# Moving the recurrent mixer of a two-block transformer kernel into the third attention

## Chip, cores and metric

One NeuronCore of one Trainium2 chip. The metric is the device time of one execution in microseconds. The engines are TensorE (PE: matmuls and transposes), VectorE (DVE), ScalarE (ACT), GpSimd (POOL) and the DMA queues, here fed by SyncE (SP). Each runs its own list of instructions in order and waits on semaphores for the others.

## What is computed

One sequence of 512 tokens of width 1024, all in float32, goes through three layers. Layers 0 and 1 add a gated residual; layer 2 is a mixer of three kinds, cut here to what the change touches.

```python
# layer 0 (even): latent attention (8 heads) and windowed attention with sinks (8 heads)
# layer 1 (odd):  differential attention (4 pairs) and forgetting attention (8 heads)
o = concat(o_a, o_b) * silu(z_gate);  x = x + gate * rmsnorm(o @ w_out, g_post)

# layer 2: sparse attention (6 heads: compressed, selected, window), stick-breaking (4 heads), recurrent (6 heads)
def hgrn2_mixer(q, f_logit, i_val, lb):            # chunks of 64 tokens
    def step(state, inp):
        b = cumsum(lf); decay = where(causal, exp(b_t - b_s), 0)
        att = einsum('bhtd,bhsd,bhtsd->bhts', qx, kx, decay)
        o = att @ vx + (qx * exp(b)) @ state
        state = exp(b_last) * state + (kx * exp(b_last - b)).T @ vx
o_hg = o_hg * rsqrt(mean(o_hg**2) + 1e-6) * hg_norm_w
mixed = concat(o_nsa * silu(nsa_z), o_sb * silu(sb_z), o_hg * silu(hg_z))
x = layer_norm(ALPHA * x + mixed @ w_out, ln_g, ln_b)
```

## The kernel before

The tokens are four tiles of 128 rows (`T = 4`). Weights come in chunks of 512 columns (2 MB) through a ring of three slots (`ring`, `ring_slots`); SyncE issues each chunk's load when the chunk that held its slot before has been used. `pr_plan` writes out the list of jobs (projections, transposes, output products) that TensorE runs in this order.

An attention (`attention(L)` on each engine) is a list of steps, one for each head and token tile: 64 steps in layer 0, 48 in layer 1, 88 in layer 2. In step v TensorE makes the scores of two steps ahead (`LOOK = 2`, two banks `SC`), transposes the weights of step v (`PT`) and multiplies those of step v - 1 with the values (`OB`). VectorE adds the mask and takes the maximum, ScalarE takes the exponential and copies the transposed weights. For differential and compressed attention VectorE also combines the weights before the transposes (semaphore `post`).

Between these, TensorE runs *fill*: projections that later stages need, cut into single products. `FILLERS[L]` lists the jobs, `SPREAD[L]` says over how many steps each few of them are dealt, and `UNITS` how many products a job counts. Half of a step's fill stands before its transposes and half behind. All fill jobs take two PSUM banks in turn (`PR`; `few` in `two_block_kernel`), so a job waits until the job two places before it has been copied out, which VectorE or ScalarE does in `tile_done`, at the end of the step in which the job ended. A gate job (`silu`) takes a clamp on VectorE, three exponentials on ScalarE (`exp_neg`) and a product on VectorE (`finish_gates`, in the next step).

In attention 1 (layer 0) the fill is a cycle of four steps: a gate tile of eight products (`gate0`), a strip of the modulation product (`adas`, its weights loaded into one slot) and the column sum of the strip before it (`adac` or `adag`). Then come the output products of the finished token tiles (`finish_tile`: two transposes `mT`, two results `y` of eight products each) and the transposed input of the next layer (`hT`). The last token tile of each layer is finished behind the attention (`last_tile`).

In layer 2 the steps are compressed, selected and window attention for token tiles 0 to 3, then the 16 stick-breaking steps. The recurrent mixer stands behind them, tile by tile: GpSimd takes the differences of the running sums for six levels of block sizes and multiplies the exponentials with keys and queries (`differences`, `operands`, 15 and 16 instructions), ScalarE takes the exponentials (`exponentials`), TensorE makes the gram products of a pair of heads (`level_products`), VectorE multiplies them with the level masks and adds the levels (seven instructions for a pair), TensorE multiplies with the values and the state (`outputs`), VectorE norms (one chain of ten instructions), and the output products of the tile before run beside it (`output_tile`). The final layer norm takes two passes on ScalarE, small steps on VectorE, and its last multiply and add on GpSimd. Below, "attention 1, 2, 3" are `attention(0)`, `attention(1)`, `attention(2)`.

## Time and profile before

| what | us |
|---|---|
| median of 3 runs | 1437.36 |
| the 3 runs | 1437.36, 1437.13, 1442.88 |
| the profiled execution, its own time | 1442.61 |
| its span (first to last instruction on the core) | 1441.1 |
| TensorE busy | 1264.0 (88%) |
| VectorE busy | 554.3 (38%) |
| ScalarE busy | 427.3 (30%) |
| GpSimd busy | 113.7 (8%) |
| stages by start: attention 1, 2, 3, stick steps, recurrent part | 194.3, 588.5, 966, 1230, 1299.8 |

Busy times overlap, so they don't add up to the span. The span says what one profiled execution took on the core; the runs' times are taken without the profiler.

### The profile page before, as it was taken

To read this page: it belongs to the slowest core of one execution; us is meant where nothing else is said; L and a number is where in the kernel's file an instruction comes from. 1 tells how busy PE (TensorE), PEld (TensorE's weight loads), DVE (VectorE), ACT (ScalarE), POOL (GpSimd) and SP (SyncE) were. 2 spreads that over 40 slices of the span, in tenths; PEclk is the share of its full clock that TensorE was granted. 3 is DMA by queue.
4 is the path that set the end of the run, shared out by engine and by line. 5 is a ranking of instruction groups with operands and counts; after the bars stand their busy time and mean duration, and the time that the engine had idled before them with its cause. 6 is when DMAs were issued, how large, how long until landed. Compare 5 with 4: busy or idle time off the path is not lost.

```text
span 1441.1 us, 15111 instructions
## 1 busy us (share of the span) xinstructions
PE 1264.0 (88%) x5264; PEld 699.6 (49%) x5264; DVE 554.3 (38%) x1422; ACT 427.3 (30%) x1086; POOL 113.7 (8%) x140
## 2 busy tenths in 40 slices
PE   4889986899998999889999989989998999856974
PEld 1555543445564444334455555555454545545541
DVE  3233322333544520334442432112125731667871
ACT  0133022334432201322234332114233533651211
POOL 0000000000001000000000000000000000484722
PEclk9989997999998999999999999989999999966986
DMA  9222334444000432322111004241101111000000
GB/s 349 92 81 64 112 117 172 146 175 118 1 1 1 117 59 59 52 67 58 59 59 59 1 11 131 59 161 44 45 0 45 44 59 59 1 0 31 1 30 29
DMA packets 60258, 99.71 MB, mean 69 GB/s; under 512 B 12068, under 2 KB 22129, under 8 KB 60184
## 3 DMA queue, kind: packets, MB, share of 16 engines
q1 hardware_dynamic: 54370, 93.58, 20.8%
q10 hardware_dynamic: 5814, 5.18, 1.1%
q8 instruction: 43, 0.70, 0.2%
q14 instruction: 31, 0.25, 0.1%
HBM read 96.60 MB, written 4.08 MB: 70 GB/s over the span
## 4 chain that ended last, share of the span: by engine, by line
PE 72%; DVE 14%; ACT 5%; issue 3%; DMA 3%; POOL 2%; ACTq 1%; DVEq 0%; SPq 0%; POOLq 0%
PE PR L856 29%; PE SC L908 6%; PE OB L886 6%; PE PT L768 6%; PE PR L768 4%; PE OB L768 4%; PE SC L768 4%; PE PT L923 3%; PE PR L949 3%; DMA ring<-in_w_ada 3%; DVE d L1661 2%; DVE stage L1661 2%; POOL arena L1569 2%; DVE tok L1661 1%; DVE arena L1877 1%
## 5 line engine op out<-in xcount | busy, mean ns | idle before, releaser
L856 PE MATMUL PR<-ring,hT 128*128 128x512 f32 (+1 forms) x784 | 381.2, 599 | 9.3 <-DVE arena L1817 6.3
L1349 ACT ACTIVATE stage<-stage,nmax 128x256 f32<-128x256 f32 (+7 forms) x200 | 103.7, 519 | 335.3 <-DVE nmax L1981 311.2
L856 PEld LDWEIGHTS PR<-ring,hT 128*128 128x128 f32 x784 | 136.3, 198 | 114.4 <-issue 98.4
L886 PEld LDWEIGHTS OB<-arena,pts 128*128 128x128 f32 (+3 forms) x880 | 132.2, 202 | 97.4 <-issue 75.9
L908 PE MATMUL SC<-arena 64*128 64x256 f32 (+15 forms) x432 | 147.5, 452 | 10.0 <-DVE nmax L1981 10.0
L856 PE MATMUL PR<-hT,ring 128*128 128x512 f32 (+1 forms) x304 | 152.8, 626 | 0.0
L1569 POOL TENSOR_TENSOR arena<-arena 128x192 f32<-128x192 f32 (+1 forms) x118 | 80.5, 683 | 826.1 <-PE OB L886 778.2
L886 PE MATMUL OB<-arena,pts 128*128 128x64 f32 (+4 forms) x880 | 131.0, 278 | 9.2 <-ACT pts L1197 9.2
L923 PEld LDWEIGHTS PT<-ident,stage 128*128 128x128 f32 (+3 forms) x440 | 58.2, 145 | 131.0 <-issue 65.1
L923 PE MATMUL PT<-ident,stage 128*128 128x128 f32 (+3 forms) x440 | 87.5, 290 | 34.7 <-ACT stage L1328 15.9
L1197 ACT ACTIVATE pts<-PT 128x256 f32<-128x256 f32 (+7 forms) x200 | 80.7, 404 | 58.4 <-issue 22.2
L1981 DVE CUSTOM_DVE_ANT_0 stage<-SC,causal 128x128 f32<-128x128 f32 (+3 forms) x96 | 47.2, 491 | 113.4 <-issue 61.4
L856 PEld LDWEIGHTS PR<-hT,ring 128*128 128x128 f32 (+1 forms) x304 | 51.6, 191 | 56.1 <-issue 54.8
L908 PEld LDWEIGHTS SC<-arena 64*128 64x128 f32 (+2 forms) x432 | 61.4, 191 | 25.4 <-DVE nmax L1981 10.4
L1981 DVE CUSTOM_DVE_ANT_0 stage<-SC,arena 128x128 f32<-128x128 f32 (+7 forms) x72 | 28.0, 388 | 116.8 <-issue 59.5
L949 PE MATMUL PR<-ring,hT 128*128 128x512 f32 x128 | 64.0, 655 | 5.9 <-DVE hT L2205 5.9
L768 PE MATMUL PR<-ring,hT 128*128 128x512 f32 (+5 forms) x160 | 48.9, 460 | 3.9 <-ACT hT L1240 2.0
L768 PE MATMUL PT<-ring,hT 128*128 128x512 f32 (+4 forms) x144 | 50.0, 502 | 0.0
L768 PE MATMUL SC<-ring,hT 128*128 128x512 f32 (+3 forms) x144 | 47.9, 490 | 0.0
L1665 DVE TENSOR_SCALAR t<-PR 128x512 f32<-128x512 f32 (+3 forms) x29 | 17.4, 600 | 73.2 <-PE PR L856 62.0
L949 PEld LDWEIGHTS PR<-ring,hT 128*128 128x128 f32 x128 | 26.1, 211 | 36.4 <-issue 30.0
L1217 ACT ACTIVATE t<-t 128x512 f32<-128x512 f32 (+3 forms) x32 | 16.8, 525 | 79.2 <-DVE t L1665 79.2
(337 smaller groups left out, 1306.6 us busy)
## 6 DMA issues: line engine op xcount, KB each, us to landing
ring<-in_w_ada SPq DMA_DIRECT2D x12, 2048.0 KB, 8.8
ring<-in_od_w_in SPq DMA_DIRECT2D x8, 2048.0 KB, 14.6
ring<-in_w_in SPq DMA_DIRECT2D x5, 1536.0 KB, 6.8
ring<-in_ev_w_in SPq DMA_DIRECT2D x3, 2048.0 KB, 7.7
ring<-in_w_in SPq DMA_DIRECT2D x3, 2048.0 KB, 9.8
ring<-in_ev_w_out SPq DMA_DIRECT2D x2, 2048.0 KB, 10.1
ring<-in_od_w_out SPq DMA_DIRECT2D x2, 2048.0 KB, 8.7
ring<-in_w_out SPq DMA_DIRECT2D x2, 2048.0 KB, 7.8
```

The costliest lines, as they stand in the source:

```text
L768: mm = pe.matmul(dst, lhs(k), rhs(k), start=(k == 0), stop=(k == K - 1))
L856: mm = pe.matmul(dst, l, r, start=(k == 0), stop=(k == KT - 1))
L886: mm = pe.matmul(ob[:, h * w:h * w + w], pts[0:rows_, v % 2, n * P:n * P + P], vb, start=(n == 0), stop=(n == len(blocks) - 1))
L908: pe.matmul(SC[s % 2][:, 0:n], q, k, start=True, stop=True).then_inc(s_done, 1)
L923: tr = pe.transpose(PT[v % 2][0:w, b * P:b * P + P], pb[:, s % NP, b * P:b * P + w], ident[:, :])
L949: mm = pe.matmul(b[:, :], hT[:, k, i * P:i * P + P], W[:, k, :], start=(k == 0), stop=(k == KT - 1))
L1197: return act.activation(dst, src, ACT.Copy, scale=scale)
L1349: give(act.activation(pb[:, s % NP, 0:n], zm[:, s % 2, 0:n], ACT.Exp, bias=nmax[:, row, c:c + 1], scale=-1.0, accum_out=rsum[:, row, c:c + ...
L1569: return pool.tensor_tensor(dst, a, b, op)
L1661: return dve.tensor_tensor(dst, a, b, op)
L1665: return dve.tensor_scalar(dst, a, s1, None, op0)
L1981: give(dve.tensor_tensor_reduce(out=z, in0=SC[s % 2][:, 0:n], in1=mask, scale=-scale, scalar=start, op0=ALU.add, op1=ALU.min, accum_out=nm ...
```

## The change

1. The recurrent mixer becomes fill of attention 3. Its jobs (`kbT`, `gram`, `ho`, `st`) and the output products of token tiles 0 to 2 go into `FILLERS[2]`; the stick steps come behind the first token tile. Gram products and level sums go head by head, the levels are added by one `tensor_reduce` over a transposed view, and the head norm, the layer norm and the exponentials become chains that advance once a step. The slot of the chunk `nz` is kept out of the ring and holds the first set of GpSimd's operands; the second set overlays the stick arrays.
2. In all three attentions VectorE's order within a step becomes: finish the gates, combine the weights, mask, and then what is left of the step before (group norms, chains, `tile_done`). Only `mT` and `hT` jobs are still handled in their own step (`URGENT`). ScalarE likewise handles the step before between its exponentials and its copy.
3. Half of each last token tile (four of eight transposes and of each result's eight products) becomes fill (`last_ahead`, `output_half`). `SPREAD` deals the fill anew.
4. The layer norm's last multiply and add of the last tile move from GpSimd to VectorE, in halves that are written out one by one.

```diff
+AHEAD = {0: 0, 1: 0, 2: 1}
+def last_ahead(L):
+    return [("mT", L, T - 1, AHEAD[L])], [("ahead", L, 0), ("ahead", L, 1)]
...
-     (("w", "hz"), [("hz", i) for i in range(T)]),
      (("w", "hq"), [("hq", m) for m in range(3)]),
-     (("w", "hi"), [("hi", i) for i in range(T)])],
+     (("w", "hi"), [("hi", i) for i in range(T)]),
+     (("w", "hz"), [("hz", 0), ("hz", 1)]),
+     (("wo", 2, 0), []),
+     (("wo", 2, 1), []),
+     (("w", "hz"), [("kbT", 0)] + grams(0, 0, 2) + [("hz", 2)] + grams(0, 2, 5) + [("hz", 3)]),
+     (("wo", 2, 1), grams(0, 5, 6) + [("ho", 0), ("st", 0), ("kbT", 1)] + grams(1, 0, 6) + finish_tile(2, 0)[:2]
+      + [("ho", 1), ("st", 1)] + finish_tile(2, 0)[2:3] + grams(2, 0, 1) + finish_tile(2, 0)[3:] + [("kbT", 2)]
+      + grams(2, 1, 2) + finish_tile(2, 1)[:3] + grams(2, 2, 3) + finish_tile(2, 1)[3:] + grams(2, 3, 6)
+      + [("ho", 2), ("st", 2), ("kbT", 3)] + grams(3, 0, 6) + [("ho", 3)] + finish_tile(2, 2)
+      + last_ahead(2)[0] + last_ahead(2)[1])],
...
-SPREAD = [[(4, 5)] + [(3, 4)] * 6 + [(5, 9), (2, 1), (4, 10), (2, 1), (2, 9), (2, 5)], [(15, 15), (4, 12), (4, 8), (2, 1), (2, 5), (2, 1), (2, 1), (2, 5)], [(21, 68), (4, 14)]]
+SPREAD = [[(4, 5)] + [(3, 4)] * 6 + [(5, 9), (2, 1), (4, 10), (2, 1), (2, 7), (2, 1), (1, 1), (2, 5)], [(15, 14), (4, 11), (1, 1), (2, 1), (2, 7), (2, 1), (2, 6), (2, 1), (2, 1), (4, 5)], [(11, 15), (12, 18), (2, 1), (2, 2), (1, 1), (1, 1), (2, 2), (1, 1), (1, 2),
+           (2, 1), (2, 1), (1, 1), (2, 1), (1, 1), (2, 1), (1, 1), (2, 3), (2, 3), (2, 1), (2, 1), (2, 3), (2, 3), (2, 1),
+           (1, 2), (2, 1), (1, 1), (1, 1), (1, 1), (2, 1), (1, 1), (1, 2), (2, 1), (1, 3), (1, 3), (1, 1), (2, 5)]]
...
+EXP_STEPS = (26, 38, 46, 56)
...
+            def level_sums(c, h):
+                b, w = take(dve, ("gram", c, h)), att[h]
+                link(tt(gm, b[:, 0:GW], levels, ALU.mult))
+                release(dve.tensor_copy(w[0:HB, HB:P], b[0:HB, GW:GW + HB]), ("gram", c, h))
+                link(dve.tensor_reduce(w[:, 0:HB], gm.rearrange("p (l t) -> p t l", l=NLEV), AX.X, ALU.add))
+                give(dve.tensor_copy(w[HB:P, HB:P], w[HB:P, 0:HB]), gs_s, HGH * c + h + 1)
...
+                def finish_behind(v, done):
+                    if late_group:
+                        finish_group(*late_group.pop(), part=1)
+                    if v >= 1 and v_units[v - 1][0] == L and last_v[L, v_units[v - 1][1]] == v - 1:
+                        finish_group(L, v_units[v - 1][1])
+                    for chain in chains:
+                        next(chain, None)
+                    for name in done:
+                        if name[0] not in URGENT:
+                            tile_done(name)
+                behind = None
                 for r_, (v, (_, g, j, sus), new) in enumerate(steps(L)):
+                    done = schedule[L][1][r_] if r_ < len(schedule[L][1]) else []
+                    finish_gates()
+                    if r_:
+                        finish_weights(v, g, sus)
                     for s in new:
...
+                    if behind:
+                        finish_behind(*behind)
+                    if urgent(done):
+                        finish_gates()
+                    for name in urgent(done):
+                        tile_done(name)
+                    behind = (v, done)
```

## Rows read from the trace of the kernel before

**Rows 1.** stages: each engine's busy us (instructions), granted clock (PEclk), DMA share.

```profile
194.30:449.60 255.30, 222.79 (x954) 124.32 (x952) 95.90 (x262) 98.51 (x272) 2.92 (x1) 0.91 0.29 96
...
588.50:859.80 271.30, 251.25 (x905) 131.12 (x903) 106.78 (x285) 84.82 (x215) 0.00 (x0) 0.98 0.17 47
...
966.00:1230.00 264.00, 252.70 (x927) 136.50 (x928) 91.98 (x282) 103.47 (x285) 0.00 (x0) 0.97 0.12 40
...
1230.00:1299.80 69.80, 50.83 (x199) 32.78 (x197) 45.64 (x68) 42.02 (x81) 46.79 (x62) 0.78 0.00 1
...
1299.80:1441.10 141.30, 100.36 (x973) 60.71 (x973) 90.98 (x189) 24.10 (x47) 59.55 (x71) 0.79 0.06 23
```

**Rows 2.** timeline, stick steps: start, us, engine, line, operation [idle before <-releaser].

```profile
1289.50 1.11 PE L923 MATMUL PT<-ident,stage 128*128 128x128 f32 x4 [7.43 <-ACT stage L1328]
```

**Rows 3.** timeline, TensorE, gram products of one pair of heads.

```profile
1316.47 1.21 PE L1116 MATMUL PT<-arena 64*64 64x64 f32 x56
```

**Rows 4.** timeline, TensorE, the last tile of attention 1.

```profile
449.65 1.08 PE L783 MATMUL SC<-ident,tok 128*128 128x128 f32 x4 [3.03 <-DVE tok L1661]
...
461.54 7.03 PE L856 MATMUL OB<-ring,hT 128*128 128x512 f32 x16
```

**Rows 5.** timeline, the end of the kernel.

```profile
1426.90 0.69 DVE L1669 SCALAR_TENSOR_TENSOR ring<-x,PR 128x512 f32<-128x512 f32 x1 [6.15 <-PE PR L949]
...
1435.45 2.34 POOL L1569 TENSOR_TENSOR x<-ring,arena 128x1024 f32<-128x1024 f32 x1
```

**Rows 6.** timeline, GpSimd, differences and products of a tile's decays.

```profile
1231.85 10.42 POOL L1569 TENSOR_TENSOR arena<-arena 128x192 f32<-128x192 f32 x15 [778.22 <-PE OB L886]
...
1286.94 11.07 POOL L1569 TENSOR_TENSOR arena<-arena 128x192 f32<-128x192 f32 x14 [4.02 <-ACT arena L1385]
...
1298.09 2.07 POOL L1569 TENSOR_TENSOR ring<-ring,arena 128x384 f32<-128x384 f32 x2
```

**Rows 7.** timeline, VectorE, level sums, head norm, and the sums again beside GpSimd.

```profile
1303.38 1.09 DVE L1661 TENSOR_TENSOR stage<-SC,grow 128x896 f32<-128x896 f32 x1 [2.19 <-PE SC L1119]
...
1304.83 1.21 DVE L1661 TENSOR_TENSOR stage<-stage 128x384 f32<-128x384 f32 x3
...
1306.08 0.61 DVE L1661 TENSOR_TENSOR ring<-stage 64x128 f32<-64x128 f32 x2
...
1314.62 0.56 DVE L2239 COPY d<-OB 128x384 f32<-128x384 f32 x1 [1.27 <-PE OB L1137]
...
1315.81 0.55 DVE L2241 TENSOR_REDUCE fr<-d 128x6 f32<-128x384 f32 x1
...
1320.44 0.75 DVE L1661 TENSOR_TENSOR tok<-tok,d 128x384 f32<-128x384 f32 x1
...
1333.71 2.05 DVE L1661 TENSOR_TENSOR stage<-stage 128x384 f32<-128x384 f32 x3
```

**Rows 8.** one stretch of attention 1, columns as in rows 1.

```profile
270.00:285.00 15.00, 11.97 (x53) 6.20 (x52) 5.29 (x14) 4.84 (x12) 0.00 (x0) 0.77 0.56 210
```

**Rows 9.** timeline, attention 1, one strip cycle.

```profile
289.89 0.69 DVE L1665 TENSOR_SCALAR t<-PR 128x512 f32<-128x512 f32 x1 [2.34 <-PE PR L856]
...
290.79 0.43 DVE L1981 CUSTOM_DVE_ANT_0 stage<-SC,causal 128x256 f32<-128x256 f32 x1 [0.21 <-PE SC L908]
...
293.48 1.05 PE L825 MATMUL PR<-pick,arena 128*128 128x1 f32 x8 [0.46 <-DVE tok L1661]
```

**Rows 10.** timeline, attention 1, other waits of TensorE.

```profile
236.24 1.93 PE L840 MATMUL PR<-ring,cond 128*32 128x512 f32 x8 [9.08 <-DMA ring<-in_w_ada]
...
313.32 2.00 PE L856 MATMUL PR<-ring,hT 128*128 128x512 f32 x2 [2.01 <-DVE arena L1817]
```

**Rows 11.** timeline, attention 2, transposes that waited for VectorE.

```profile
614.99 0.33 PE L923 MATMUL PT<-ident,stage 128*128 128x128 f32 x1 [2.58 <-DVE stage L1669]
...
627.45 0.69 PE L923 MATMUL PT<-ident,stage 128*128 128x128 f32 x2 [4.21 <-DVE stage L1669]
...
730.93 0.66 PE L923 MATMUL PT<-ident,stage 128*128 128x128 f32 x4 [0.98 <-DVE stage L1669]
```

More of the change, by code:

```diff
@@ L123, with grams @@
          ("gate0", 1, 3)]
+def grams(c, first, end):
+    return [("gram", c, h) for h in range(first, end)]
 FILLERS = [
@@ L194, in last_tile @@
     def last_tile(L):
-        jobs.extend(finish_tile(L, T - 1))
+        jobs.append(("mT", L, T - 1, 1 - AHEAD[L]))
+        jobs.extend(("y", L, T - 1, h) for h in range(2))
         chunk_end[("wo", L, 0)] = chunk_end[("wo", L, 1)] = len(jobs)
@@ L302, in ring_slots @@
             continue
+        if "nz" in kept and turn % RING == kept["nz"]:
+            turn += 1
         slots[c] = turn % RING
@@ L313 @@
 NP = 4
-HG_EARLY = (78, 84)
+EXP_STEPS = (26, 38, 46, 56)
 LOOK = 2
@@ L959, in last_tile @@
                     pe.wait_ge(pt_ev[r], (sum(e[0] <= L for e in v_units) + 1 - r) // 2)
-                for name in finish_tile(L, T - 1):
-                    whole_tile(name)
+                late = 1 - AHEAD[L]
+                whole_tile(("mT", L, T - 1, late))
+                for h in range(2):
+                    for _ in output_half(L, h, late):
+                        pass
                 for i in LEFT[L]:
@@ L1167, in _ @@
-            for _ in output_tile(T - 1):
-                pass
+            last_tile(2)
         @block.scalar
@@ new lines, in carry_state @@
+            def carry_state(c):
+                b = take(dve, ("st", c))
+                for m in range(3):
+                    for r in range(2):
+                        q = slice(MN * r, MN * r + MN)
+                        src = b[q, m * P + MN * r:m * P + MN * r + MN]
+                        dst = state[m][q, MN * r:MN * r + MN]
+                        if c == 0:
+                            ins = dve.tensor_copy(dst, src)
+                        else:
+                            ins = stt(dst, dst, dec[c % 2][q, m:m + 1], src, ALU.mult, ALU.add)
+                        if (m, r) != (2, 1):
+                            link(ins)
+                release(ins, ("st", c))
@@ L2266, in _ @@
-            output_tile(T - 2)
-            mixed_half(T - 1)
-            residual_half(T - 1, 0)
-            residual_half(T - 1, 1)
-            output_tile(T - 1)
+            for chain in chains:
+                for _ in chain:
+                    pass
+            i, c = T - 1, slice(6, 7)
+            residual_half(i, 0)
+            residual_half(i, 1)
+            hear(ln_q, "ln_q")
+            say(ts(lam[:, 7:8], ss[:, 4:5], ss[:, 5:6], ALU.add, -1.0 / D, ALU.mult), ln_m, "ln_m")
```

616 lines of the change are left out of this document (324 added, 292 removed).

## The prediction

> **What bounds the kernel now.** I read the stages first [rows 1]: the reader is to see that TensorE is busy for 223 of 255 us of attention 1, 251 of 271 us of attention 2 and 253 of 264 us of the first part of attention 3, that it falls to 51 of 70 us in the stick steps that end attention 3, and to 100 of 141 us in the recurrent part behind them, at a mean granted clock of 0.79. So until 1230 us TensorE's queue sets the time, and a wait anywhere on it is paid in full. From 1230 us on a chain over the other engines does. In the stick steps TensorE waits for ScalarE's last exponential, once for 7.43 us [rows 2]; in the recurrent part VectorE is busy 91 of 141 us, and most of that lies between TensorE's products and the next ones.
>
> What TensorE would need at full clock is busy time times clock by stage [rows 1]: 252.7 x 0.97 = 245 us, 50.8 x 0.78 = 40 us and 100.4 x 0.79 = 79 us, in all 364 of the 475 us from 966 us to the end. 111 us there are waits and low clock: that is what the change can win from. Attention 1 and 2 hold 32 and 20 us of waits.
>
> **Part 1: the recurrent mixer as fill of attention 3.** All of it but the last tile's second half moves into the 88 steps of attention 3; the stick steps come after the first token tile instead of last, with some five products of fill in each. TensorE's work is the 364 us and two additions. The gram products are made head by head, so only two column halves of the array work at once, where before two row halves did too. The 56 records of a pair of heads took 1.21 us [rows 3], 15 to 18 us in all with their tails. If half the overlap is lost that doubles; if the queue's pace of issue was the limit, nothing changes. I take +6 of 0 to 18, since 28 products in 1.21 us are 43 ns each, nearer to a pace of issue than to four full streams. The output products are split by block, some 30 more: +3. 373 us.
>
> Added to it is what no fill covers. The last tile: the final group's finish 3.0 us as in attention 1 [rows 4], transposes and copy 1.5 us; its eight remaining products are in the 373 (such 16 records take 7.03 us [rows 4]). The end: before, 14.2 us pass from the last product at 1426.9 us to 1441.1 us [rows 5]; two GpSimd operations, the second of 2.34 us, go, two VectorE halves of 0.69 us come, and the multiplication by the gain runs beside the squares. 9.6 us stay. With 3 us of low clock: 17 us.
>
> Then the waits inside the fill, which I read off the order of jobs. *GpSimd:* the second tile's operands overlay the stick arrays, so its differences start after step 33: 10.4 us, then ScalarE's exponentials over three steps, then 11.1 + 2.1 us of products [rows 6]: some 30 us until the transposes of step 43, where TensorE has 24 us of work. 6 us. The third and fourth tile come out even within 2 us. *VectorE:* for a pair of heads it pays 1.09, a copy, 1.21 and 0.61 us, from 1303.38 to 1306.69 us [rows 7], 1.65 us a head. After the change: 0.55 us (half of 1.09), a copy, one strided sum, a copy. A sum over 384 elements takes 0.55 us [rows 7], so 0.65 us for 448; a strided view could make it up to twice that, 24 x 0.65 = 16 us of VectorE more, which is why both ends stay in the range. I take 1.75 us a head. Steps 64 to 75 hold eight heads (14 us), two head norms of 5.6 us (from 1314.62 to 1321.2 us, less a wait for ScalarE [rows 7]), twelve masks of 0.65 us, two group finishes and a state: 41 us of VectorE against 29 us of TensorE, 12 us lost. Steps 36 to 49: 46 against 42 us, mostly inside GpSimd's 6 us; +2. Elsewhere two gram tiles share two banks that are given back one step later: 5 us. Opening and stick steps: 6 us. The 2 to 3% that attention 3's first part loses between its instructions: 5 us. Low clock: a wait of 2.3 us stands in a stretch of 15 us at a mean of 0.77 [rows 8]; for some six such: 12 us. In all 48 us. Were all of it covered by the step of slack that masks have, 5 us would stay.
>
> 373 + 17 + 48 = 438 us for 475 us: **-37 us**. From the bounds of the terms (work 373 to 388, waits 22 to 75): -63 to +5.
>
> The page "VectorE: DVE Perf Modes" of the Trainium skill (Rules for kernel authors) calls tensor_reduce the slowest VectorE operation and advises to restructure it on a hot path. By the row it costs what an addition of 384 elements does, and the term stays at 0.65 us; by the rule the four additions, 0.9 us a head, would have been kept.
>
> GpSimd's work moves beside attention's. The same three additions take 1.21 us with GpSimd idle and 2.05 us beside it [rows 7]. Some 20 us of such operations, a quarter of them beside GpSimd, make 4 us, which I hold to be inside the 12 us above. The page "SBUF — State Buffer" of the Trainium skill (Who interferes with whom) says that a VectorE instruction with two SBUF inputs contends with GpSimd's reads; by that rule, the trace agrees.
>
> **Part 2: masks first, everything else a step later.** VectorE and ScalarE handle what the fill finished one step later, behind the masks of the next. In attention 1 this costs. Each strip cycle has gate, strip and column sum in two banks: the sum waits for the gate's bank, the next gate for the strip's. Before, the gate's clamp starts at 289.89 us, right when its products end, and the sum waits 0.46 us [rows 9]. After, the clamp waits for the next scores and their mask (0.43 us at 290.79 [rows 9]): 1.4 us later, 1.9 us where the window heads add an operation. The next gate then waits for scores, mask (0.5) and strip copy (0.7): 1.3 us where it waited none, 0.8 more where it already waits 2.01 us [rows 10]. The second cycle's strip waits 9.08 us for a transfer [rows 10], which swallows the delay before it. Left: five sums x 1.6, three gates x 1.4, three x 0.8: 14.6 us. With low clock behind waits of 2 us [rows 8], +8. Behind the waiting product stand the step's transposes, values and next scores, so nothing hides it. **+22 us**, 5 if other slack covers it, 30 at most.
>
> In attention 2 it wins: five waits of the transposes for VectorE's combined weights, the first 2.58, the longest 4.21, the last 0.98 us, 11.2 us in all [rows 11], go, because weights come first, and masks, forget chain and group norm behind. One or two low stretches with them, 3 us; a late gate bank costs 1.5 back: **-12 us** (-6 to -15).
>
> **Part 3: half of the last tiles early.** In attention 1 eight products (7.0 us) move into the last five steps, where TensorE idles about 3 us, and their transposes with them: **-4 us**. In attention 2 TensorE is busy to the end: -1.
>
> **Sum.** 1441.1 - 37 + 22 - 12 - 4 - 1 = 1409 us of span. The profiled execution's own time is 1442.61 us, 1.5 above its span and 5.2 above the median of 1437.36, so the median would be 1409 + 1.5 - 5.2 = 1405. VectorE's queue has a step of slack that I counted only in part, worth some 3 us: **1402**.
>
> **Rivals.**
> A, mine: 1402, from 1385 to 1425. Chance 0.46.
> B, the fill hides more: waits of 22 + 17 us on 376 of work make 415 for 475, -60; the strips' delay is half covered, +10; with -12 and -5: 1441 - 67 - 3.7 = 1370. For it: VectorE would be busy about half of attention 3. Against it: the order of jobs leaves light steps that hold heads alone. Chance 0.32.
> C, slower: the two banks of the fill decide. Every small job (24 grams, 4 norms, 7 transposes and states, 7 copies, 6 results: 48) gives its bank back only after the next mask. If each made TensorE wait 1.4 us, and every second one were followed by 1 us of low clock, that is 91 us where I have 48: 373 + 17 + 91 = 481 for 475, +6, and 1441 + 6 + 22 - 17 - 3.7 = 1448. From about 1.2 us a job on the whole change is slower; the waits for a bank are 0.46 us in [rows 9] and 2.01 us in [rows 10]. Chance 0.12 (1431 to 1465).
> D, gain and loss cancel: the strided sum takes double and the array's halves don't overlap, +16 and +12 on mine: 1430 to 1440. Chance 0.10.
>
> Faster by over 0.5% (below 1430): A, B and 0.03 of D, 0.81. Within 0.5%, what a measurement can't tell from no change: 0.07 of D and 0.02 of C, 0.09. Slower: 0.10. The range reaches over B and A and into D: 1362 to 1433.
>
> **What would show it.** Right: attention 1 longer by about 20 us, its column sums waiting some 2 us for VectorE and each next gate for the strip's copy; attention 2 without waits of transposes for VectorE's weights; stick steps with TensorE full; TensorE waiting at the second tile's transposes for GpSimd and around the fourth tile's grams for VectorE; 10 us from the last product to the end, with no GpSimd operation. Wrong: attention 1 unchanged (the late handling is covered), attention 3 dense throughout (then B), or TensorE waiting before most small jobs (then C).

## The result: slower by 8.6%, with the profile after

The kernel after takes 1564.03 us (median, 1561.59 to 1569.35), the kernel before 1440.12 us (1437.13 to 1444.85) on the same chip: 1.0862 times as long, with a 95% interval of 1.0816 to 1.0909. The prediction said 1402 us, with a range of 1362 to 1433.

The stages come first. The columns of the windows are the stretch, its length, each engine's busy us (instructions), TensorE's mean granted clock (PEclk), the DMA share and GB/s. The first two rows answer to the first two of [rows 1]; the others are attention 3 with the recurrent mixer in it: first token tile, stick steps, the rest, and the end.

```profile
194.30:480.30 286.00, 243.14 (x974) 134.92 (x972) 97.28 (x267) 99.51 (x275) 2.09 (x1) 0.87 0.26 86
615.60:917.80 302.20, 270.07 (x925) 141.65 (x924) 107.75 (x288) 85.41 (x216) 0.00 (x0) 0.93 0.15 42
1019.50:1127.20 107.70, 105.26 (x302) 51.91 (x303) 19.73 (x78) 29.16 (x91) 0.00 (x0) 0.98 0.09 30
1127.20:1234.30 107.10, 91.80 (x368) 53.46 (x367) 75.10 (x119) 54.98 (x108) 24.94 (x31) 0.91 0.14 50
1234.30:1537.70 303.40, 265.05 (x1460) 172.27 (x1458) 129.18 (x344) 82.18 (x209) 71.31 (x99) 0.69 0.05 16
1537.70:1559.00 21.30, 11.23 (x20) 4.75 (x20) 5.17 (x11) 3.69 (x9) 0.00 (x0) 0.66 0.07 25
```

Attention 1 grew by 31 us, attention 2 by 31, and what stands behind 1019.5 us takes 539.5 us, where before it took 475.1. In the long row TensorE is busy for 265 of 303 us, and its clock is 0.69. The same view, cut where the granted clock changes, shows what that mean is made of:

```profile
1265.80:1334.00 68.20, 56.47 (x336) 41.30 (x336) 31.26 (x79) 16.90 (x44) 29.67 (x47) 0.50 0.08 29
1334.00:1405.70 71.70, 62.05 (x298) 33.44 (x297) 26.29 (x78) 21.17 (x55) 24.18 (x34) 0.83 0.02 8
1405.70:1487.60 81.90, 71.85 (x426) 51.27 (x426) 40.89 (x106) 17.25 (x51) 4.70 (x2) 0.50 0.02 7
```

Two stretches, 150 us together, stand at 0.50 throughout, which is 1.2 GHz, although TensorE is busy for 128 us of them. They hold the grams of the second token tile, and two of the third's with all of the last's.

Now the waits. In attention 1 and then attention 2, what TensorE waited for (us in total, times, longest us):

```profile
PE PR L973 <- DVE arena L1958: 13.7, 6, 3.3
PE PR L948 <- DVE tok L1738: 5.9, 3, 2.1
PE PR L941 <- DVE tok L1738: 5.8, 3, 2.1
```

```profile
PE PR L973 <- DVE arena L1983: 9.9, 3, 5.4
PE PR L973 <- DVE arena L1980: 7.0, 3, 3.1
PE PR L973 <- ACT arena L1237: 5.2, 1, 5.2
PE PR L823 <- DVE tok L1738: 4.4, 1, 4.4
```

Of attention 3 to the end, the first two lines are:

```profile
PE PR L848 <- DVE grow L1783: 9.7, 4, 3.0
PE PR L973 <- ACT arena L1237: 8.4, 1, 8.4
```

The first group is what the prediction described: the next gate (L973) waits for the strip's copy, the column sums (L948, L941) for the gate's clamp. In the second group the transposes of [rows 11] no longer wait, but other fill products do, for longer. In the third, grams (L848) wait for the copies of earlier grams and other jobs: 10 of the 24, 19.9 us in all, where own_step_all below has 2 such waits of 3.7 us together. The timeline shows the longest of the second group (start, us, engine, line, operation, [idle before <-releaser]), with VectorE's queue in front of it:

```profile
763.49 0.59 PE L1044 MATMUL SC<-arena 64*128 64x512 f32 x2
...
769.49 2.05 PE L973 MATMUL PR<-ring,hT 128*128 128x512 f32 x2 [5.40 <-DVE arena L1983]
```

```profile
764.22 0.69 DVE L2166 CUSTOM_DVE_ANT_0 stage<-SC,causal 128x512 f32<-128x512 f32 x1 [11.08 <-PE SC L1044]
...
764.95 0.69 DVE L2166 CUSTOM_DVE_ANT_0 stage<-SC,causal 128x512 f32<-128x512 f32 x1
...
766.48 0.69 DVE L1738 TENSOR_TENSOR d<-d,rr 128x512 f32<-128x512 f32 x1
767.20 0.69 DVE L1738 TENSOR_TENSOR d<-d,subln 128x512 f32<-128x512 f32 x1
767.93 0.69 DVE L1738 TENSOR_TENSOR tok<-tok,d 128x512 f32<-128x512 f32 x1
768.65 1.42 DVE L1983 COPY arena<-PR 128x512 f32<-128x512 f32 x2
```

TensorE's next fill job needs a bank. The products in that bank ended at 748.1 us, but their copy (L1983) now stands behind the next step's two masks and behind the finish of a group. Those masks wait for scores that TensorE itself has just issued (VectorE idles 11 us ahead of them). So the bank can't come back before TensorE has been through its scores and VectorE through everything in front of the copy.

**Whole-kernel accounting.** The table below is worked out from the traces. A part goes from the first score product of an attention to its last value product (which is why attention 1 and 2 are some us off the windows above), the last one from attention 3's first score to the end. "Idle" is time in which TensorE runs no product and no weight load; "at 1.2 GHz" is busy time in stretches at the lower clock, half of which is lost; "work" is busy time times clock. All are of the profiled execution. Each ratio is to the kernel before as it ran beside that kernel on the same chip, where its median was between 1440.12 and 1445.39 us, so it isn't the quotient of two medians of this table.

| kernel | median us | ratio to before (95%) | attention 1 | attention 2 | attention 3 to end | idle | at 1.2 GHz | work |
|---|---|---|---|---|---|---|---|---|
| before | 1440.12 | | 251.9 | 279.4 | 476.4 | 71.6 | 65.7 | 371.9 |
| after | 1564.03 | 1.0862 (1.0816 to 1.0909) | 283.2 | 310.1 | 543.2 | 68.6 | 182.5 | 383.4 |
| own_step_12 | 1499.45 | 1.0374 (1.0354 to 1.0394) | 256.0 | 279.3 | 540.8 | 69.2 | 175.8 | 383.7 |
| own_step_all | 1458.20 | 1.0082 (1.0067 to 1.0097) | 256.4 | 279.3 | 496.2 | 46.3 | 131.0 | 384.5 |
| gram_pairs | 1445.97 | 1.0017 (1.0004 to 1.0029) | 252.7 | 279.3 | 486.1 | 55.3 | 116.9 | 372.4 |
| pairs_by_additions | 1457.88 | 1.0110 (1.0088 to 1.0132) | 256.7 | 279.2 | 497.1 | 63.4 | 123.9 | 371.8 |
| mixed_dealing | 1460.29 | 1.0124 (1.0104 to 1.0144) | 256.7 | 279.4 | 500.0 | 66.0 | 116.0 | 376.0 |
| dense_in_grams | 1586.04 | 1.0969 (1.0937 to 1.1001) | 286.7 | 310.1 | 565.1 | 62.5 | 190.8 | 407.2 |
| dense3_in_grams | 1501.15 | 1.0396 (1.0357 to 1.0434) | 257.2 | 278.9 | 537.5 | 49.1 | 69.4 | 453.6 |
| thin_grams | 1455.54 | 1.0081 (1.0066 to 1.0096) | 256.4 | 279.0 | 496.5 | 51.2 | 105.2 | 392.7 |
| before_weights_first | 1435.41 | 0.9931 (0.9905 to 0.9958) | 251.9 | 272.4 | 473.7 | 65.3 | 74.2 | 371.3 |
| before_norm_too | 1433.38 | 0.9917 (0.9899 to 0.9935) | 252.6 | 272.6 | 469.0 | 60.7 | 74.0 | 371.3 |
| before_late_jobs | 1462.77 | 1.0151 (1.0131 to 1.0171) | 278.2 | 272.6 | 473.7 | 64.3 | 77.5 | 370.6 |

Idle, time at 1.2 GHz and work are those of the last part. Attention 1 and the opening differ by 4 us between profiled executions of kernels with the same code there (252.7 and 256.7 us), by how long a stretch at 1.2 GHz is; differences of that size there mean nothing.

### The profile page after: what moved, and what is told of

Read it like the earlier page. It is cut to its first block, busy times and chain, and to the rows that moved or that the text cites. A ratio compares the mean times of both kernels' runs of the same rounds, so it can differ in the third digit from the quotient of the medians.

```text
span 1559.0 us, 15278 instructions
## 1 busy us (share of the span) xinstructions
PE 1361.0 (87%) x5315; PEld 767.0 (49%) x5315; DVE 555.5 (36%) x1437; ACT 428.8 (28%) x1093; POOL 103.6 (7%) x138
## 4 chain that ended last, share of the span: by engine, by line
PE 59%; DVE 8%; issue 5%; ACT 2%; POOL 1%; ACTq 1%; DVEq 0%; POOLq 0%
PE PR L973 26%; PE SC L1044 7%; PE OB L1022 6%; PE PR L808 4%; PE PR L991 3%; PE PT L1059 3%; PE OB L808 2%; PE SC L808 2%; PE PR L848 2%; DVE d L1738 1%; PE PT L808 1%; PE PR L823 1%; DVE tok L1738 1%; POOL arena L1651 1%; PE PR L865 0%
## 5 line engine op out<-in xcount | busy, mean ns | idle before, releaser
L973 PE MATMUL PR<-ring,hT 128*128 128x512 f32 (+1 forms) x864 | 435.2, 626 | 34.4 <-DVE arena L1958 13.7
L973 PEld LDWEIGHTS PR<-ring,hT 128*128 128x128 f32 x864 | 161.4, 207 | 176.9 <-issue 151.1
L1022 PEld LDWEIGHTS OB<-arena,pts 128*128 128x128 f32 (+2 forms) x880 | 141.2, 215 | 92.4 <-issue 82.7
L973 PE MATMUL PR<-hT,ring 128*128 128x512 f32 (+1 forms) x304 | 144.3, 613 | 17.1 <-ACT arena L1237 13.7
L1022 PE MATMUL OB<-arena,pts 128*128 128x64 f32 (+3 forms) x880 | 141.6, 293 | 7.2 <-ACT pts L1237 2.7
L1059 PEld LDWEIGHTS PT<-ident,stage 128*128 128x128 f32 (+2 forms) x440 | 62.3, 155 | 91.2 <-issue 82.1
L1059 PE MATMUL PT<-ident,stage 128*128 128x128 f32 (+2 forms) x440 | 94.1, 308 | 2.7 <-DVE stage L1738 2.7
L973 PEld LDWEIGHTS PR<-hT,ring 128*128 128x128 f32 (+1 forms) x304 | 53.0, 188 | 82.3 <-issue 80.6
L1651 POOL TENSOR_TENSOR ring<-arena 128x192 f32<-128x192 f32 (+1 forms) x30 | 17.9, 595 | 690.6 <-DVE arena L2042 688.3
L808 PE MATMUL PR<-ring,hT 128*128 128x512 f32 (+4 forms) x176 | 61.6, 506 | 1.9 <-DVE hT L1743 1.9
L808 PE MATMUL SC<-ring,hT 128*128 128x512 f32 (+4 forms) x160 | 49.4, 467 | 0.0
L808 PEld LDWEIGHTS PR<-ring,hT 128*128 128x128 f32 x176 | 31.9, 198 | 28.5 <-issue 23.2
L1651 POOL TENSOR_TENSOR arena<-arena 128x192 f32<-128x192 f32 (+1 forms) x62 | 38.2, 616 | 81.7 <-ACT arena L1324 59.2
```

Source lines behind the costliest of these rows:

```text
L808: mm = pe.matmul(dst, lhs(k), rhs(k), start=(k == 0), stop=(k == K - 1))
L973: mm = pe.matmul(dst, l, r, start=(k == 0), stop=(k == KT - 1))
L1022: mm = pe.matmul(ob[:, h * w:h * w + w], pts[0:rows_, v % 2, n * P:n * P + P], vb, start=(n == 0), stop=(n == len(blocks) - 1))
L1059: tr = pe.transpose(PT[v % 2][0:w, b * P:b * P + P], pb[:, s % NP, b * P:b * P + w], ident[:, :])
L1651: return pool.tensor_tensor(dst, a, b, op)
```

## The experiments

**own_step_12.** The kernel after, with the delay taken out of attention 1 and 2, on VectorE and on ScalarE (the loops that call `urgent` are changed to match):

```diff
-def urgent(done):
+OWN_STEP = (0, 1)
+def urgent(L, done):
-    return [name for name in done if name[0] in URGENT]
+    return [name for name in done if L in OWN_STEP or name[0] in URGENT]
```

> The kernel after, but in attention 1 and 2 VectorE and ScalarE finish every fill job in its own step again (still behind that step's masks, and weights still first); attention 3 as it is. Theory (what attention 1 and 2 lost is the bank given back a step later, and the low clock behind those waits): attention 1 falls from 286 us to 251-262, attention 2 from 302 to 258-272, attention 3 with the recurrent part stays at 535-545, total 1500-1515. Rival (it is the order of masks and weights, or how evenly the fill is dealt): attention 1 and 2 stay above 280 and 295 us, total 1550-1570.

Measured: 1499.45 us, attention 1 at 256.0 and attention 2 at 279.3 us, the last part at 540.8. The theory holds (its total is missed by half a us). Both attentions are back to what the kernel before has, but for the 4 us of the note above, and 60 of the 118 us of span are explained. Attention 2's 279.3 by the table is 271 in the windows' terms, inside the theory's range.

**own_step_all.** The same with `OWN_STEP = (0, 1, 2)`.

> As the kernel with jobs in their own step in attention 1 and 2, and now in attention 3 too, grams, head norms and states included. Theory (attention 3 with the recurrent part is slow because TensorE works there at 1.2 GHz on stretches of small products, and the waits come second): that part stays within 15 us of 539.5 us, TensorE's busy time at half clock stays above 140 us; total 1485-1515. Rival (the waits for the two banks set off the low clock, so without them it goes): that part falls below 500 us with less than 90 us at half clock, total below 1470.

Measured: 1458.20 us, the last part at 496.2 us. The rival came closer than the theory in two of its three numbers: without the late banks idle time fell by 23 us and busy time at 1.2 GHz by 45, and the part by 45 us, three times what the theory allowed. But 131 us stay at 1.2 GHz, more than the rival said. The windows of this kernel show where:

```profile
1206.30:1264.30 58.00, 55.38 (x333) 40.99 (x334) 30.31 (x80) 16.72 (x44) 29.46 (x47) 0.50 0.07 26
1264.30:1339.40 75.10, 70.53 (x484) 42.95 (x482) 40.72 (x115) 29.82 (x76) 25.12 (x34) 1.00 0.02 8
1339.40:1387.20 47.80, 40.65 (x245) 27.81 (x244) 26.94 (x69) 8.22 (x27) 4.68 (x2) 0.50 0.03 12
```

In the first TensorE is busy for 55 of 58 us, at half clock; its one wait there is of 2.62 us for GpSimd (another of 2.2 us, for ScalarE, ends as the stretch begins). In the second it is busy for 70.5 of 75 us at full clock. What differs is the work: the second holds the output products of 128x512 between the grams, while the first has only four records of them, at its end. The same is true of every stretch of over 15 us at 1.2 GHz in this part of the kernels after, own_step_all, gram_pairs and mixed_dealing: of 95 to 426 records each, none to four are of 128x512. In the traces the two only go together; the runs with added products below try whether one makes the other.

**before_late_jobs.** The converse: the kernel before, weights first (below), and in attention 1 alone the jobs finished a step later.

```diff
+                    if L < 1:
+                        if behind:
+                            finish_behind(*behind)    # group finish, chains, jobs of the last step
...
+                        behind = (v, done)
+                        continue
```

> The kernel before with the weights first (1435.4), and one more edit in attention 1 alone: VectorE and ScalarE finish all fill jobs but the transposes one step later, behind the next masks, as the kernel after does; dealing, bank order and everything else as before. Theory (that alone is what attention 1 lost): attention 1 grows from 252 to 272-282 us with 2 us of wait at each column sum, and the rest stays, total 1456-1466. Rival (the delay only costs with the kernel after's other edits, its dealing and half of the last tile early): attention 1 grows by less than 8 us, total below 1444.

Measured: 1462.77 us, attention 1 at 278.2 us where the same kernel without the delay has 251.9. The theory holds. TensorE's waits in attention 1 are, with the delay:

```profile
PE PR L857 <- DVE arena L1840: 13.7, 6, 3.3
...
PE PR L833 <- DVE tok L1684: 5.9, 3, 2.1
PE PR L826 <- DVE tok L1684: 5.8, 3, 2.1
```

and without it (before_weights_first):

```profile
PE PR L856 <- DVE arena L1817: 6.3, 3, 2.3
...
PE PR L832 <- DVE tok L1661: 2.2, 3, 1.0
...
PE PR L825 <- DVE tok L1661: 1.5, 3, 0.7
```

The three lines with the delay are those of the kernel after to a tenth of a us. So the delay, with the old dealing and the old last tile, makes 26.3 us, nearly all of attention 1's loss. (The edit also puts the gates' finish ahead of the masks; own_step_12 has that too, and loses nothing by it.)

**gram_pairs.** own_step_all, and the products of two heads interleaved into two banks as before.

```diff
-            def level_products(c, h):
-                m, r = h // 2, h % 2
-                b = begin(("gram", c, h))
+            def level_products(c, m):
+                banks = [begin(("gram", c, 2 * m + r)) for r in range(2)]
                 for l in range(NLEV):
                     for j in range(2):
+                        for r, b in enumerate(banks):
```

> The kernel with jobs in their own step in all three attentions, and the gram products of two heads issued as one interleaved row of 30 into the two banks again, as the kernel before did it (the dealing is redrawn for whole pairs, over the same steps). Theory (the split by head lost the overlap of the array's two row halves: one head takes 1.14 us at full clock and 1.96 us at half, where before a pair took 1.15 and 1.97): attention 3 with the recurrent part loses 12 x 1.14 = 13.7 us of work and falls from 496 to 470-484 us, total 1432-1446. Rival (VectorE's level sums, 2 us a head, are what paces these steps): TensorE waits by as much as it gains, total 1452-1462.

Measured: 1445.97 us; work fell by 12.1 us and the part by 10.1, to 486.1 us. So the theory holds for the work and the total and misses the part by 2 us. The rest of the sum is that idle time rose by 9.0 us and the loss to the lower clock fell by 7: grams now wait for two banks at once, 15.6 us in all where own_step_all has 3.7. The rival was right that VectorE's level sums hold these steps up, but not that they take the whole gain. The timelines show the price of a gram directly. One head in own_step_all, at 1.2 GHz (30 records, 1.97 us from first start to last end):

```profile
1223.48 1.76 PE L851 MATMUL PR<-arena 64*64 64x64 f32 x28
...
1225.03 0.42 PE L852 MATMUL PR<-arena 64*64 64x64 f32 x2
```

Two heads in gram_pairs at 2.4 GHz (60 records, 1.15 us):

```profile
1258.81 0.93 PE L849 MATMUL PR<-ring 64*64 64x64 f32 x48 [0.23 <-DVE tok L1752]
...
1259.53 0.33 PE L849 MATMUL PR<-arena 64*64 64x64 f32 x8
...
1259.65 0.31 PE L852 MATMUL PR<-ring 64*64 64x64 f32 x4
```

By the trace, all single heads that ran wholly at 2.4 GHz took 1.11 to 1.14 us and at 1.2 GHz 1.93 to 1.97 us; in the kernel before the pairs that stand alone took 1.15 and 1.97 us. A head alone costs what a pair costs.

**dense_in_grams and dense3_in_grams.** Do the small products hold the clock down? One dense product ahead of each gram job in the kernel after, and three ahead of each in own_step_all:

```diff
                 b = begin(("gram", c, h))
+                freed(pe, ("hi", T - 1))
+                for _ in range(1):        # range(3) in the second
+                    pe.matmul(b[:, :], a2["hi"][:, 0, 0:P], a2["hi"].rearrange("p i n -> p (i n)")[:, 0:512],
+                              start=True, stop=True)
```

> The kernel after, and before the 15 small products of each of the 24 gram jobs one more product of 128 columns by 512, into the same bank, which the grams then overwrite: it adds work and computes nothing. Theory (the steps that hold small products alone are what TensorE's clock falls on): 24 x 0.55 = 13 us of work more, but busy time at half clock in attention 3 with the recurrent part falls from 182 us to below 90, that part from 539.5 to 490-515 us, total 1525-1545. Rival (waits of 2 to 3 us set the clock, whatever the products are): the stretches at half clock stay as long, the part grows by 13 to 26 us, total 1575-1590.

> The kernel with jobs in their own step in all three attentions, and three dense products of 128 columns by 512 ahead of each gram job's 15 small ones (work added, nothing computed; one such product before each moved nothing in the kernel after). Theory A (the small products hold the clock down; enough dense work between them raises it): 24 x 3 x 0.55 = 40 us of work more, but busy time at half clock in attention 3 with the recurrent part falls from 131 us to below 70, that part 496 to 500-512 us, total 1462-1475. Theory B (something else than the kind of product holds it down): busy time at half clock stays above 120 us or grows, that part 536 us or more, total above 1495.

Measured: with one, 1586.04 us and 191 us at 1.2 GHz (182.5 without): nothing gained, as the rival said. With three, 1501.15 us and 69.4 us at 1.2 GHz, where own_step_all has 131.0. The clock came up as theory A said, but the part (537.5 us) and the total lie where theory B had them, because the work costs nearly twice what I had put: 69 us of work for 72 products, 0.96 us each for 0.55. That was my misreading: the profile counts two records for one such product (16 records for eight in [rows 4]). The two runs differ in the late banks too, so they don't say by themselves that one product a gram is too few. Where own_step_all stood at 0.50 and behind it, the windows with three read

```profile
1216.20:1260.00 43.80, 36.84 (x273) 22.03 (x271) 21.30 (x53) 7.80 (x22) 18.58 (x30) 0.81 0.08 25
1260.00:1350.00 90.00, 85.16 (x432) 47.56 (x431) 36.32 (x99) 28.92 (x73) 34.93 (x49) 0.92 0.02 7
```

**thin_grams.** The other way round, on own_step_all: one dense product (as in dense_in_grams) in place of 12 of the 15 small ones. Its result is not the reference's, since it leaves out six of the levels.

```diff
-                for l in range(NLEV):
+                for l in range(NLEV - 1, NLEV):
```

> The kernel with jobs in their own step in all three attentions, with work left out: of the 15 small products of each gram job the 12 of the first six levels are left out, and one dense product of 128 columns by 512 fills the bank in their place, so the output is not the reference's. Theory A (the small products hold the clock down): about 24 x 0.35 = 8 us less work, and busy time at half clock in attention 3 with the recurrent part falls from 131 us to below 70; that part 445-465 us, total 1408-1428. Theory B (waits and the rest of these steps hold it down): busy time at half clock stays above 110 us; that part 480-490 us, total 1440-1452.

Measured: 1455.54 us, the part at 496.5 us, 105.2 us at 1.2 GHz: the clock between the theories, the time above both. Work rose by 8 us in place of falling by 8, by the same misreading of the dense product. So the grams are at most a part of what goes with the low clock; attention's own value products (128x64) and those of the head outputs fill the same steps, and no run varies them.

**mixed_dealing.** gram_pairs with the dense products dealt among the grams, at no added work:

```diff
-     (("w", "hi"), [("hi", i) for i in range(T)]),
-     (("w", "hz"), [("hz", 0), ("hz", 1)]),
+     (("w", "hi"), [("hi", 0), ("hi", 1)]),
...
+     (("w", "hz"), [("kbT", 0)] + grams(0, 0, 2) + [("hz", 0)]),
+     (("w", "hi"), [("hi", 2)] + grams(0, 2, 4) + [("hi", 3)] + grams(0, 4, 6)),
+     (("w", "hz"), [("ho", 0), ("st", 0), ("kbT", 1)] + grams(1, 0, 2) + [("hz", 1)] + grams(1, 2, 4) + [("hz", 2)]
+      + grams(1, 4, 6) + [("hz", 3)]),
```

> The kernel with own steps and gram pairs, with the same work dealt anew in attention 3: the last two value tiles and all four gate tiles of the recurrent mixer (48 dense products) are held back from steps 15 to 32 and put between the gram pairs of the first two token tiles (steps 33 to 49), some three a step; the later gram steps have none to take, since no dense product is left that is ready. Theory (dense products beside the small ones keep the clock up, and this time at no added work): the low stretches of the first and second tile's grams (54 us of gram_pairs' 117 us at half clock) shrink to below 20 us, that part 486 to 465-475 us, total 1424-1436. Rival (the stick steps, thinned out, wait for their exponentials and forget chains instead, and fall to the lower clock there): that part 483-495 us, total 1443-1455.

Measured: 1460.29 us, the part at 500.0 us, 116.0 us at 1.2 GHz as in gram_pairs, idle up by 11 us and work, by the new dealing, by 3.6. The rival's mechanism holds, 5 us above its range. The two long stretches over the first two tiles' grams, 27.3 us each, became one of 27.3 and one of 13.7 us, but others of 3 to 17 us came in the thinned-out stick steps and behind, and the sum is the same. The dense products dealt are 384 wide. Between 1169.1 and 1199.8 us 40 records of them stand beside two pairs' grams, and only 3.4 us are at 1.2 GHz; in the 27.3 us that follow there are 11, and all of it is.

**pairs_by_additions.** gram_pairs with the strided sum undone:

```diff
-                link(dve.tensor_reduce(w[:, 0:HB], gm.rearrange("p (l t) -> p t l", l=NLEV), AX.X, ALU.add))
-                give(dve.tensor_copy(w[HB:P, HB:P], w[HB:P, 0:HB]), gs_s, HGH * c + h + 1)
+                link(tt(gm[:, 0:3 * HB], gm[:, 0:3 * HB], gm[:, 3 * HB:6 * HB], ALU.add))
+                link(tt(gm[:, 0:HB], gm[:, 0:HB], gm[:, HB:2 * HB], ALU.add))
+                link(tt(gm[:, 2 * HB:3 * HB], gm[:, 2 * HB:3 * HB], gm[:, 6 * HB:7 * HB], ALU.add))
+                link(tt(w[0:HB, 0:HB], gm[0:HB, 0:HB], gm[0:HB, 2 * HB:3 * HB], ALU.add))
+                give(tt(w[HB:P, HB:P], gm[HB:P, 0:HB], gm[HB:P, 2 * HB:3 * HB], ALU.add), gs_s, HGH * c + h + 1)
```

> The kernel with own steps and gram pairs, with each head's level sum made by the kernel before's additions (three of 128 rows, and the last on each half) in place of the one strided sum and its copy. Theory (the strided sum takes 0.92 us with a copy of 0.24 behind it, the additions some 0.25 to 0.35 us each, and VectorE isn't what paces the gram steps): within 3 us of the pairs' 1446, either way. Rival (the strided sum holds VectorE's queue and so the banks): 6 to 12 us faster, 1434-1440.

Measured: 1457.88 us, 12 us slower than gram_pairs (the last part 11.0): neither. The theory took the two ways to cost about the same, the rival took the strided sum to be the dear one. The groups of VectorE's instructions (busy us, mean ns, idle before) say otherwise. Additions:

```profile
L1744 DVE TENSOR_TENSOR d<-d 128x64 f32<-128x64 f32 x48 | 15.2, 317 | 1.7
...
L1744 DVE TENSOR_TENSOR d<-d 128x192 f32<-128x192 f32 x24 | 10.2, 425 | 0.8
L1744 DVE TENSOR_TENSOR grow<-d 64x64 f32<-64x64 f32 x32 | 9.5, 296 | 1.1
...
L1744 DVE TENSOR_TENSOR ring<-d 64x64 f32<-64x64 f32 x16 | 3.5, 220 | 0.5
```

Strided sum, in gram_pairs:

```profile
L1790 DVE TENSOR_REDUCE grow<-d 128x64 f32<-128x448 f32 x16 | 14.7, 921 | 0.5
...
L1790 DVE TENSOR_REDUCE ring<-d 128x64 f32<-128x448 f32 x8 | 7.3, 916 | 0.3
...
L1791 DVE COPY grow<-grow 64x64 f32<-64x64 f32 x16 | 5.3, 332 | 0.6
```

38.4 us over 24 heads are 1.60 us a head, against 0.92 for the sum and 0.2 to 0.33 for its copy. Head by head, five short operations lose to one long one. And the 0.4 us a head show up in the time almost one for one (24 x 0.4 = 9.6 us, and the part grew by 11.0), so VectorE does pace these steps.

That isn't the whole comparison. The kernel before adds the levels for two heads at once, in five operations a pair:

```profile
L1661 DVE TENSOR_TENSOR ring<-stage 64x128 f32<-64x128 f32 x24 | 10.0, 417 | 0.8
L1661 DVE TENSOR_TENSOR stage<-stage 128x128 f32<-128x128 f32 x24 | 9.9, 411 | 0.8
L1661 DVE TENSOR_TENSOR stage<-stage 128x384 f32<-128x384 f32 x12 | 8.0, 670 | 0.4
```

That is 27.9 us for the same 24 heads, partly beside GpSimd, and the sum with its copies takes 28.8 us in gram_pairs. Additions pair by pair inside the fill were not tried.

**before_weights_first and before_norm_too.** Two parts of the change alone, on the kernel before: the combined weights ahead of the next masks, and then the last tile's final norm without GpSimd as well.

```diff
                 for r_, (v, (_, g, j, sus), new) in enumerate(steps(L)):
+                    if r_:
+                        finish_weights(v, g, sus)
                     for s in new:
```

```diff
+                if i == T - 1:
+                    dve.wait_ge(ln_in, 32)
+                    link(stt(x[:, i, :], yb, lam[:, 7:8], lng, ALU.add, ALU.mult))
                 hear(sq_s, "sq_s")
                 rsqrt(ss[:, 0:1], 1, D, LN_EPS)
+                if i == T - 1:
+                    for h in range(2):
+                        w = slice(512 * h, 512 * h + 512)
+                        give(stt(x[:, i, w], x[:, i, w], rr[:, 0:1], lnb[:, w], ALU.mult, ALU.add), out_s, h + 1)
+                    return
```

> The kernel before with one edit: VectorE makes the combined weights of a step (attention 2's differences, attention 3's compressed branch) ahead of the next masks, all else as before. Theory (the five waits of TensorE's transposes for the weights, 11 us, go): attention 2 falls from 271 to 258-264 us, total 1426-1434. Rival (the masks come later by as much, and TensorE waits at the scores or behind them): attention 2 stays at 268-274 us, total 1436-1444.

> The kernel before with the weights ahead of the masks, and the last tile's final norm on VectorE alone, as the kernel after has it (multiplication by the gain beside ScalarE's squares, result in two halves, each with its own store). Theory: the end after the last product, 14.2 us in the kernel before, falls to 9-11 us, total 3 to 5 us below the kernel with weights first alone (1435.4): 1430-1433. Rival (VectorE has to finish the gain before it can help with the root, or the two stores cost what the operations give): 1434-1437.

Measured: 1435.41 and 1433.38 us, 0.7% and 0.8% below the kernel before on the same chip. With the weights first, attention 2 falls from 279.4 to 272.4 us and the last part by 2.7 us. In the windows' terms attention 2 is at 264.3 us, just above the theory's 258 to 264, and the total lies between theory and rival. The waits for the weights do not all go: of 11.6 us 6.6 stay, and most of that is one wait.

```profile
624.12 0.51 ACT L1349 ACTIVATE stage<-stage,nmax 128x256 f32<-128x256 f32 x1 [13.47 <-issue]
...
626.45 0.44 PE L923 MATMUL PT<-ident,stage 128*128 128x128 f32 x2 [4.17 <-DVE stage L1669]
```

VectorE waits there for ScalarE's exponentials, and ScalarE's queue has been issuing transfers since 613.2 us: putting the weights first on VectorE left this wait at 4.17 us, where it was 4.21. With the norm on VectorE too, the time from the last product to the end falls from 14.3 to 9.7 us, as expected, and the recurrent part with the end from 141.3 to 136.2 us in the profiled execution. before_norm_too is the fastest kernel of this study. Its interval overlaps with that of the kernel with weights first alone, so the norm's own 2 us in the medians aren't resolved.

## Why the prediction was wrong, by its own steps

**The steps that failed** are two terms of the sum, and either alone would have turned the sign: the price of a bank given back a step late, outside attention 1, and the low clock of the mixer's steps.

The first, the late banks. For attention 3 the prediction has "two gram tiles share two banks that are given back one step later: 5 us" and "Low clock: ... 12 us"; for attention 2 "a late gate bank costs 1.5 back". own_step_all against own_step_12 prices the first at 44.6 us, 23 us of waits and 22 of the clock that goes with them. own_step_12 against the kernel after prices attention 2's at 30.8 us, 17 of waits and 13.5 of clock. I had seen the mechanism: I worked it out for attention 1 and gave it to rival C for attention 3. C, with 12 in 100 from me, names the right mechanism, but neither its number (1448, at most 1465) nor what it would have been known by came: TensorE waited before 10 of the 24 grams, not before most small jobs. That C stands 43 us above my own sum, close to the 44.6 measured, is luck: it has 48 waits of 1.4 us, where taking the late banks out gave back 23 us of idle time, nearly as much again of clock, and another 31 us in attention 2, where C priced nothing.

The second, the clock: "Low clock: ... 12 us", with 3 at the end, for all of attention 3 and the mixer. own_step_all, where no bank is late, loses 65 us to it (half of 131.0). The last part misses its forecast by 104 us: 50 are this clock, 42 the late banks, 11.5 work. By its own row the term was small as well, since 12 us busy at 0.77 lose 2.8 us, and six such 16.5; and [rows 1] had shown 0.79 where the same products ran before.

**Attention 1**, +22: right, in mechanism and nearly in size. 26.3 us on the kernel before alone, 27.2 us in the kernel after. The waits of 2 us at the sums and 1.3 to 3.3 us at the gates are those forecast; idle time rose by 16 us where I had put 14.6, and the clock took 11 where I had put 8.

**Attention 2**, -12: weights first alone is worth 7.0 us, 5.0 of waits and 1.7 of clock. I had taken all five waits for waits on VectorE's order; the longest, 4.21 us, is for ScalarE, whose queue is full of transfer issues, and it stays. The 31 us of the late banks turned the sign. I had looked at the order of the weights and the gate's bank only, and not asked, for each fill job of attention 2 (fq, fk, ff, fv), what stands ahead of its copy in the new order; the 5.4 us wait above is such a copy.

**Part 1, work**, +6 of 0 to 18 for the grams: mis-sized. The split by head lost the row halves' overlap altogether: 12.1 us by gram_pairs. The argument "28 products in 1.21 us are 43 ns each, nearer to a pace of issue" was wrong: the 56 records of [rows 3] are 28 products of a pair, and the 28 records of one head's 14 take nearly as long, so the two row halves had run at once. Work in all rose by 11.5 us (371.9 to 383.4), forecast 9. Its base of 364 us was 7 too low: it multiplies each stage's busy time by the stage's mean clock, but much of the time at 1.2 GHz is idle. From 966 us on TensorE is busy for 403.9 us, 65.7 of them at the lower clock, so 371 us at full clock. The bounds have a slip and a gap: 364 + 18 + 3 is 385 and not 388, and the waits' 22 and 75 are nowhere worked out.

**Part 1, waits inside the fill** (48 us with low clock): without late banks idle time is 46.3 us, where the forecast's terms without the clock and the banks come to 45 (36 - 5 in the fill, 14 at the end). GpSimd held up the second tile's transposes by 2.6 us, not 6. What did not follow is the clock, as said: 65 us lost where the kernel before loses 33. So even with own steps and pairs the recurrent mixer as fill does not pay here: 486.1 us for 476.4.

**The strided sum**, 0.65 us a head, bound at twice that: 0.92 measured, and with the multiplication (0.62) and the copies 2.0 us a head on VectorE, not 1.75. The additions, which the prediction has at 0.9 us a head, cost 1.60 when made head by head. The page "VectorE: DVE Perf Modes" of the Trainium skill (Rules for kernel authors) advises to restructure a tensor_reduce on a hot path. Restructured head by head, that cost 12 us here; in pairs, as the kernel before has it, the additions cost VectorE as much as the sum and its copies (27.9 and 28.8 us), and no run tries them in the fill.

**The end**: 9.6 us forecast from the last product, 9.3 us found. The timeline, answering to [rows 5]:

```profile
1539.56 10.15 PE L991 MATMUL PR<-ring,hT 128*128 128x512 f32 x16 [0.75 <-ACT hT L1237]
...
1551.68 1.28 DVE L1746 SCALAR_TENSOR_TENSOR x<-tok,lam,hT 128x1024 f32<-128x1024 f32 x1
...
1554.64 1.54 DVE L1746 SCALAR_TENSOR_TENSOR x<-x,rr,hT 128x512 f32<-128x512 f32 x2
```

No GpSimd operation, and the gain beside the squares. The products ahead of it took 10.15 us for the 7.03 of [rows 4], because the granted clock was 0.50 until 1545.7 us.

**Part 3**, half of the last tiles early, -4 and -1: little or nothing. From attention 1's first score to attention 2's takes 383.6 us in both own_step_12 and the kernel before. Over all profiled executions it takes 383.6 to 384.5 us with the old last tile and 380.2 to 384.4 with the new one and own steps, so at most some 2 us of the 4 are there on average. From attention 2's first score to attention 3's it takes 379.4 us in before_weights_first and in own_step_12: nothing. The products left the stretches between and stand in the attentions. It wasn't tried alone.

**The sum of the span**, 1441.1 to 1559.0: late jobs 60.4 us (attention 1 and 2, with 2.4 us behind) and 44.6 (attention 3), lost overlap 10.1, what is left of moving the mixer 9.7, in all 124.8; weights first give 7 back in attention 2. (These are differences of the table's parts; those of whole spans differ by up to 5 us, by the opening.) That attention 2 still lasts 279.3 us by the table is the early half of its last tile, which left the stretch behind it shorter by as much (100.0 us for 106.9).

**Open.** What keeps TensorE at 1.2 GHz there, which is 50 of the 104 us by which the last part missed. Three dense products a gram raised the clock (131.0 to 69.4 us). One a gram changed nothing in the kernel with late banks, one in place of most of the gram gave 105.2 us, and dealing the existing ones among the grams moved the low stretches without shortening their sum.

## What to carry to other kernels

When a change moves the work that gives a buffer back behind other work in a queue, price it for every job that shares the buffers, not for the one cycle that is easy to see: the first few in each stage, the instruction that waits, and all that now stands ahead of the copy. Keep the release of a shared bank in the step in which its products end; order alone (weights before masks) can be changed without it, and that was the part that paid. Before moving products next to others, ask which halves of the array ran at once in the old order, and what the granted clock was where the engine did the same kind of work. Before counting a wait as won by a new order, follow it to the engine that really ends it.

## What the hardware showed that I had not expected

- TensorE busy for 55.4 of 58.0 us at a granted clock of 0.50, in steps of products of 64x64x64, 128x64 and 64x256; 70.5 of 75.1 us at 1.00 right behind it, with 128x512 products between (own_step_all). The page "TensorE: Matmul & The Clock Gate" of the Trainium skill (Part 1: The HAM clock gate) says that the slow clock is the default and activity releases it; the trace shows that in the second stretch and not in the first.
- Two heads' 30 products of 64x64x64 on the two row halves take the time of one head's 15: 1.15 us against 1.14 at 2.4 GHz, 1.97 against 1.97 at 1.2 GHz.
- Waits took the clock with them: taking 23 us of waits out of attention 3 took 45 us of busy time out of the lower clock, 22 us of time.
